# Turning the block-attention heads in 32x32 squares on VectorE, and moving one weight split, in a hybrid decoder block

## What is computed

```python
o_gla  = rms_norm(gla_chunked(...), gla_out_gain) * silu(gr)
o_moba = rms_norm(moba_attention(q_m, k_m, v), moba_out_gain)
x = x + concatenate([o_gla, o_moba]) @ w_out
h = rms_norm(x, norm2_gain)
x = x + (silu(h @ w_ffn_gate) * (h @ w_ffn_up)) @ w_ffn_down
return rms_norm(x, final_norm_gain)
```

## Time and profile before

| what | value |
|---|---|
| median of 3 runs | 301.15 us (300.92 to 301.44) |
| profiled execution | 301.26 us, of which the span of the trace is 299.5 us |
| TensorE busy | 292.4 us, 98% of the span |
| VectorE busy | 241.9 us, 81% |
| ScalarE busy | 170.4 us, 57% |
| GpSimd busy | 17.4 us, 6% |
| mean granted TensorE clock | 0.996 |

### The profile page before, as it was taken

One profiled execution on the slowest core, in us unless ns is written; L12 is line 12 of the kernel. 1 busy time (PEld: TensorE's weight loads), 2 busy tenths in 40 slices (PEclk: granted clock), 3 DMA queues, 4 the chain that ended last, 5 costly groups with the idle time before them and its releaser, 6 DMA issues.

```text
span 299.5 us, 4024 instructions
## 1 busy us (share of the span) xinstructions
PE 292.4 (98%) x1373; PEld 242.8 (81%) x1373; DVE 241.9 (81%) x402; ACT 170.4 (57%) x244; POOL 17.4 (6%) x41
## 2 busy tenths in 40 slices
PE   8999999999999999999999999999999999999992
PEld 7878888888898888888888888888888888888881
DVE  1999999877889687988888888888898978787155
ACT  3979798979765887717171718080808080813123
POOL 5210100000021001300000000000000000000011
PEclk9999999999999999999999999999999999999998
DMA  7997837837767122393939292929292929030003
GB/s 253 331 320 257 257 97 280 230 120 276 276 189 244 60 82 69 108 317 101 320 94 328 85 337 81 340 67 353 59 354 63 361 56 364 22 123 0 0 0 140
DMA packets 37382, 55.49 MB, mean 185 GB/s; under 512 B 2982, under 2 KB 26618, under 8 KB 37370
## 3 DMA queue, kind: packets, MB, share of 16 engines
q1 hardware_dynamic: 37204, 55.16, 54.6%
q10 hardware_dynamic: 166, 0.17, 0.2%
HBM read 53.75 MB, written 1.57 MB: 185 GB/s over the span
## 4 chain that ended last, share of the span: by engine, by line
PE 96%; DVE 1%; issue 1%; POOL 1%; ACT 0%; POOLq 0%; DVEq 0%
PE acc L515 15%; PE acc L517 15%; PE acc L516 15%; PE aux L517 13%; PE aux L516 13%; PE aux L515 13%; PE aux L618 1%; PE acc L532 1%; PE acc L569 1%; PE acc L572 1%; PE acc L575 1%; PE aux L688 1%; PE aux L541 1%; DVE x_sb L1388 1%; PE aux L712 1%
## 5 line engine op out<-in xcount | busy, mean ns | idle before, releaser
L1151 DVE TENSOR_TENSOR w_lo<-raw,w_hi 128x2048 fp32r<-128x2048 f32 x46 | 103.3, 2286 | 15.3 <-ACT w_hi L882 15.2
L882 ACT CAST w_hi<-raw 128x2048 fp32r<-128x2048 f32 x46 | 86.0, 1908 | 6.5 <-DMA raw<-in_w_in 2.9
L515 PE MATMUL aux<-w_hi,aT_hi 128*128 128x512 f32 (+1 forms) x180 | 69.7, 387 | 0.0
L517 PE MATMUL aux<-w_hi,aT_lo 128*128 128x512 f32 (+1 forms) x180 | 69.6, 387 | 0.0
L516 PE MATMUL aux<-w_lo,aT_hi 128*128 128x512 f32 (+1 forms) x180 | 69.6, 387 | 0.0
L1454 DVE STREAM_TRANSPOSE reuse_c<-reuse_c 32x128 f32<-32x128 f32 x160 | 48.4, 303 | 2.4
L1094 ACT CAST pT_hi<-reuse_c 128x512 fp32r<-128x512 f32 x10 | 6.2, 621 | 72.9 <-DVE reuse_c L1454 72.9
L515 PE MATMUL acc<-w_hi,aT_hi 128*128 128x512 f32 x118 | 47.1, 399 | 0.0
L517 PE MATMUL acc<-w_hi,aT_lo 128*128 128x512 f32 x118 | 46.0, 390 | 0.0
L516 PE MATMUL acc<-w_lo,aT_hi 128*128 128x512 f32 x118 | 46.0, 390 | 0.0
L515 PEld LDWEIGHTS aux<-w_hi,aT_hi 128*128 128x128 f32 x180 | 33.8, 188 | 6.9
(11 more groups left out here) (203 smaller groups left out, 283.8 us busy)
## 6 DMA issues: line engine op xcount, KB each, us to landing
raw<-in_w_ffn_gate SPq DMA_DIRECT2D x22, 512.0 KB, 4.0
raw<-in_w_ffn_up SPq DMA_DIRECT2D x22, 512.0 KB, 5.3
raw<-in_w_ffn_down SPq DMA_DIRECT2D x22, 512.0 KB, 5.9
raw<-in_w_in SPq DMA_DIRECT2D x20, 512.0 KB, 5.1
raw<-in_w_out SPq DMA_DIRECT2D x8, 512.0 KB, 4.4
raw<-in_w_in SPq DMA_DIRECT2D x8, 256.0 KB, 4.7
x_sb<-in_x SPq DMA_DIRECT2D x2, 512.0 KB, 3.8
m_moves<-reuse_c SPq DMA_DIRECT2D x1, 512.0 KB, 3.4
```

What stands on the lines that cost most here:

```text
L515: nc.tensor.matmul(dst, left_hi[:, k, tok], right_hi, start=first, stop=False)
L517: return nc.tensor.matmul(dst, left_lo[:, k, tok], right_hi, start=False, stop=last)
L882: nc.scalar.copy(w_hi[:, slot % RING, :], raw[:, slot % RAW, :]).then_inc(hi_ready, 1)
L1151: nc.vector.tensor_tensor(w_lo[:, slot % RING, :], raw[:, slot % RAW, :], w_hi[:, slot % RING, :].bitcast(f32), ALU.subtract).then_inc(lo_ ...
```

## The change

The eight TensorE transposes of the block-attention heads are gone. VectorE turns the squares of both tiles right after `normed`, ahead of split 15. For tile 0, ScalarE copies 8 blocks of 32x128 and GpSimd the other 8; for tile 1, ScalarE copies 12 and GpSimd 4. ScalarE makes the high parts and VectorE the low parts from SBUF, in new places of their orders. GpSimd's second inverse root comes behind its copies. Split 16 goes behind the block-attention heads on ScalarE, and behind the low part of gated tile 0 on VectorE. VectorE's wait for both activated gates becomes one wait for each tile.

```diff
+M_HEADS_MOVED_BY_POOL = (8, 12)
...
+        m_head_squares = reuse_e[:, 0:1024].rearrange("p (t c h i) -> p t c h i", t=T, c=QUADS, i=SQUARE)
+        m_headsT = reuse_e[:, 1024:2048].rearrange("p (t h s) -> p t h s", t=T, h=HEADS)
...
 # GpSimd
+            def move_m_heads(t, groups):
+                pool.wait_ge(m_heads_turned, t + 1)
+                for g in groups:
+                    for c in range(QUADS):
+                        nc.gpsimd.tensor_copy(m_headsT[SQUARE * c:SQUARE * (c + 1), t, :, SQUARE * g:SQUARE * (g + 1)],
+                                              m_head_squares[SQUARE * g:SQUARE * (g + 1), t, c, :, :]).then_inc(m_heads_by_pool, 1)
+                pool.wait_ge(m_heads_by_pool, M_HEADS_MOVED_BY_POOL[t])
+
+            head_root(0)
+            move_m_heads(0, (0, 1))
+            move_m_heads(1, (0,))
+            head_root(1)
...
 # TensorE
-                      9: [probs_transposed], 10: [moba_outputs, gla_updates], 11: [gla_outputs, lambda: heads_transposed(0, (3, 0))]}
+                      9: [probs_transposed], 10: [moba_outputs, gla_updates], 11: [gla_outputs]}
...
 # ScalarE
             split(15)
-            split(16)
...
+            def take_m_headsT(t):
+                act.wait_ge(m_heads_by_act, t + 1)
+                act.wait_ge(m_heads_by_pool, M_HEADS_MOVED_BY_POOL[t])
+                nc.scalar.mul(aT_hi[:, 0:HEADS, t * P:(t + 1) * P], m_headsT[:, t, :, :],
+                              gains[:, MOBA_ROW:MOBA_ROW + 1]).then_inc(headsT_hi_ready, 1)
...
+            move_m_heads(0, (2, 3))
             act.wait_ge(tile0_in_psum, len(BLOCKS))
             take_r(0)
+            take_m_headsT(0)
             act.wait_ge(ms_h_ready, 1)
             for t in range(T):
                 act.wait_ge(gla_in_psum, t + 1)
                 nc.scalar.activation(squares[:, t * W:(t + 1) * W], aux[:, 1 + t, :], ACT.Square).then_inc(sq_ready, 1)
-            take_headsT(0, (3, 0))
+            move_m_heads(1, (1, 2, 3))
             act.wait_ge(unit_used, IN_UNITS)
             take_r(1)
+            take_m_headsT(1)
+            split(16)
             split(17)
...
 # VectorE
                 normed(0, t, bank, o_moba[:, t, :, :]).then_inc(heads_ready, 1)
+            for t in range(T):
+                dve.wait_ge(heads_ready, t + 1)
+                nc.vector.transpose(m_head_squares[:, t], o_moba[:, t, :, :].rearrange("p h (c i) -> p c h i", c=QUADS)
+                                    ).then_inc(m_heads_turned, 1)
...
             split(15)
+            take_m_headsT(0)
             head_squares(1)
...
-            take_headsT(0, (3, 0))
-            split(16)
             dve.wait_ge(rstd_h_ready, 2)
-            dve.wait_ge(silu_r_ready, 2)
             normed(1, 0, 1, o_gla[:, 0, :, :])
             then(normed(1, 1, 2, o_gla[:, 1, :, :]))
             for t in range(T):
+                dve.wait_ge(silu_r_ready, t + 1)
                 nc.vector.tensor_tensor(o_gla[:, t, :, :], o_gla[:, t, :, :], silu_r[:, t, :, :], ALU.mult).then_inc(heads_ready, 1)
+            take_m_headsT(1)
...
             take_gla_headsT(0)
+            split(16)
             split(17)
```

More of the change, by code:

```diff
@@ L293, in build_block @@
         heads_ready = sem("heads_ready")
-        headsT_in_psum = sem("headsT_in_psum")
+        m_heads_turned = sem("m_heads_turned")
+        m_heads_by_act = sem("m_heads_by_act")
+        m_heads_by_pool = sem("m_heads_by_pool")
         heads_turned = sem("heads_turned")
@@ L489, in _, with head_root @@
             nc.gpsimd.memset(reuse_b[:, :], 0.0).then_inc(a_zeroed, 1)
-            for group in range(2):
+            def head_root(group):
                 pool.wait_ge(ms_h_ready, group + 1)
@@ L717, in gla_outputs @@
                     last.then_inc(gla_in_psum, 1)
[L719 to L724, removed]
             def out_product(t, group, n):
@@ L1001, in _, with move_m_heads @@
             split(15)
-            split(16)
[L1003 to L1010, removed]
+            def move_m_heads(t, groups):
+                act.wait_ge(m_heads_turned, t + 1)
+                for g in groups:
+                    for c in range(QUADS):
+                        last = nc.scalar.copy(m_headsT[SQUARE * c:SQUARE * (c + 1), t, :, SQUARE * g:SQUARE * (g + 1)],
+                                              m_head_squares[SQUARE * g:SQUARE * (g + 1), t, c, :, :])
+                last.then_inc(m_heads_by_act, 1)
+            def take_m_headsT(t):
[3 more added lines that the diff above has]
+                              gains[:, MOBA_ROW:MOBA_ROW + 1]).then_inc(headsT_hi_ready, 1)
             def take_r(t):
@@ L1343, in _, with take_m_headsT @@
                 normed(0, t, bank, o_moba[:, t, :, :]).then_inc(heads_ready, 1)
+            for t in range(T):
+                dve.wait_ge(heads_ready, t + 1)
+                nc.vector.transpose(m_head_squares[:, t], o_moba[:, t, :, :].rearrange("p h (c i) -> p c h i", c=QUADS)
+                                    ).then_inc(m_heads_turned, 1)
+            def take_m_headsT(t):
+                dve.wait_ge(headsT_hi_ready, t + 1)
+                dst = slice(0, HEADS), slice(t * P, (t + 1) * P)
+                lo_of_scaled(aT_lo[:, dst[0], dst[1]], m_headsT[:, t, :, :], gains[:, MOBA_ROW:MOBA_ROW + 1],
+                             aT_hi[:, dst[0], dst[1]]).then_inc(headsT_lo_ready, 1)
             split(15)
+            take_m_headsT(0)
             head_squares(1)
             nc.vector.tensor_scalar(ms_h[:, 1, :], ss_h[:, 1, :], 1.0 / DV, EPS, ALU.mult, ALU.add).then_inc(ms_h_ready, 1)
[L1348 to L1358 removed]
             dve.wait_ge(rstd_h_ready, 2)
[L1360 removed]
             normed(1, 0, 1, o_gla[:, 0, :, :])
```

8 lines of the change are left out of this document (removed).

## The result

| | before, same chip | after |
|---|---|---|
| median of 4 runs | 301.04 us | 306.19 us (306.00 to 306.46) |
| profiled execution | 301.26 us, span 299.5 | 306.00 us, span 303.9 |

The change makes the kernel slower: ratio 1.0166, 95% interval 1.0154 to 1.0178, or about 5.1 us. The sign and the mechanism are the forecast ones, the size is not: 2.8 us were forecast, and the time lies outside the range of 302.7 to 305.2.

A forecast was written before the change was run, and what follows sets the result against it. TensorE, 96% of the chain, was taken to bound the kernel: 0.87 us taken out, waits of 1.59, 1.29, 0.24, 0.29 and 0.27 put in, net +2.81, so 301.26 becomes 304.1 us, range 302.7 to 305.2.

The forecast's parts named there:

- The sign and the mechanism: Whole kernel: slower (chance 0.89), through held GpSimd with copies of 0.15 to 0.30 us, +2.3 to +3.6 us (chance 0.60).
- GpSimd's price: Tile 0's eight GpSimd copies: 0.20 us each, three before split 15, five from 88.51 to 89.51.
- The dearer rival at 0.29: GpSimd's tile 0 copies: two before the split, six left until 90.3; +3.6 us, 304.8; dearer copies had chance 0.10.
- ScalarE's queue: Ahead of the third block: ScalarE full from 91.23, gated tile 0's copies from about 99.7, TensorE starting at 103.52.
- my habit of the rows: Back-to-back instructions on one engine: the next starts about 0.09 us before the last has ended.
- The hold: Beside split 15: GpSimd instructions reading SBUF wait while VectorE subtracts two SBUF tensors, so five copies wait until 88.51.
- the slow root beside three splits: Profile before: GpSimd's one-element root took 2.49 us at 123.35 beside VectorE's splits, against 0.56 at 116.56.
- The deadlines: Starts of the four out_product blocks and tile 1's first gate product: slack before of 0.75, 5.5, 1.07, 0.95, 0.68 us.
- The rival by which only the first wait is real: Second low part not dependent in time on the gated norm: sum from -0.2 to +0.7 us, chance 0.07.
- The one by which GpSimd is not held: Tile 0's GpSimd copies not held or nearly free: high part at 88.70, +1.9 us, 303.2, chance 0.17.
- the later load: Unit 19's load: goes at about 105.7 instead of 92.55, lands by 111, wanted at 119.73 at the earliest, no cost.
- the later split 16: Split 16, ready at 105.7, is needed by the first gate product only after 115, so costs nothing.

The follow-up runs named there:

- split16_act_back: The changed kernel with ScalarE's split 16 back behind split 15, VectorE's order as changed: 305.32 us, ratio 1.0140 to the kernel before.
- split15_behind: The changed kernel with VectorE's split 15 moved behind the low part of block-attention tile 0: 305.49 us, ratio 1.0149 to the kernel before.
- split16_alone: The kernel before with only split 16 moved to its new places on ScalarE and VectorE, TensorE transposes kept: 300.98 us, ratio 0.9993.
- both_splits: The changed kernel with VectorE's split 15 behind tile 0's low part and ScalarE's split 16 back behind split 15: 306.15 us, ratio 1.0163 to the kernel before.
- gpsimd_half: The changed kernel with 4 of tile 0's copies on GpSimd and 12 on ScalarE, instead of 8 and 8: 305.64 us, ratio 1.0149 to the kernel before.

## Why the prediction was right in kind and short in size

The waits first. A wait is how much later a block starts than it would behind the block before it: 5.44 us after that, or, for the gate product, 11.73 (118.44 - 106.71). The first is counted from 90.39 - 0.87 - 0.34 = 89.18, as TensorE reaches the gated outputs 0.34 earlier in the profile after (83.74 for 84.08).

| wait at | forecast | measured | by the starts after |
|---|---|---|---|
| first block | 1.59 | 2.78 | 91.96 - 89.18 |
| second | 1.29 | 1.32 | 98.72 - 97.40 |
| third | 0.24 | 0.74 | 104.90 - 104.16 |
| fourth | 0.29 | 0.23 | 110.57 - 110.34 |
| gate product | 0.27 | 0.27 | 122.57 - 122.30 |
| sum | 3.68 | 5.34 | |

5.34 - 0.87 - 0.34 = 4.13, the lateness at the gate product. Two waits are mis-sized, the first by 1.19 and the third by 0.50; three are right. The table says when TensorE started, and not what each wait cost: a larger first wait leaves less for the next ones. What sets the end is the third block and what comes behind it.

*The step that failed: GpSimd's price.* "I take 0.20, as such instructions overlap a little", and from it three copies before the split and five held, done at 89.51. Measured: 0.28 to 0.30 each and 0.34 from start to start; two free, one held through the split, five behind it, done at 90.27. They don't overlap, they stand 0.06 apart. VectorE begins this stretch 0.16 earlier in the profile after (83.65 for 83.81), so the high part, forecast at 89.60, began at 90.36 + 0.16 = 90.52: 0.92 of the 1.19. Five copies at 0.34 instead of 0.20 make 0.7 of it; the rest is mostly that the held copy ends 0.16 after the split. A further 0.18 is that TensorE had come 0.34 earlier and VectorE only 0.16, and 0.10 is the restart below. The dearer rival at 0.29 had the number of copies right and forecast 304.8; it had no time between them.

The rows for a better price were there, but not for the right one. The select reads and writes and took 0.29; the memset only writes. Of the overlap the whole timeline before says, one row ahead of the select shown:

```profile
3.25 0.29 POOL L460 TENSOR_SCALAR_AFFINE_SELECT tri_mid<-tri_mid 128x128 fp32r<-128x128 f32 x1
```

Selects start 0.24 to 0.25 apart (3.25, 3.49, 3.74). At 0.25 five held copies would end at 89.76, and the sum at 304.3. No row before has the 0.34. The copies raise a semaphore each and these selects do not; whether that makes the difference was not tested.

*The second failed step, at the third wait: ScalarE's queue.* From the high part of tile 0 to the gated copies 10.14 were summed (89.60 to about 99.7) and 10.35 measured (90.36 to 100.71): the two squarings 0.10 more, the twelve copies 0.05, the two splits 0.10. Then the high part of gated tile 0 began 0.09 after its last copy had ended (100.71 + 2.45 = 103.16 against 103.25), where my habit of the rows had it 0.09 before: it waits for copies of its own engine. The sum itself lost 0.08 in rounding: 99.74 + 2.44 is 102.18, not 102.1. That is how 0.92 at tile 0 became 1.40 at the low part of gated tile 0 (104.01 + 0.75 + 0.16 = 104.92 for 103.52). That this queue is the releaser was shown by split16_act_back, and the chain runs through it; the single joins were only read from the timeline.

*TensorE's restart.* After each wait the first matmul began 0.10 to 0.15 after the low part had ended (91.96 against 91.11 + 0.75). I had let it start at once. A block that starts after a pause also takes 5.57 (91.96 to 97.30 + 0.23) instead of 5.44; the table counts these 0.13 with the next wait.

*The hold was right.* Reading the slow root beside three splits as a GpSimd instruction held by VectorE's subtraction came true in its place: 2.24 for one copy under split 15, none of twelve held where no split ran beside them. The Trainium skill's SBUF — State Buffer, section "Who interferes with whom", names this pair, and the trace agrees. The Trainium skill's GPSIMD Engine Reference, section "Performance versus the Vector engine", would have made a copy cheaper still than my 0.20; here the measured 0.34 decides.

*The deadlines were right, in order and in releaser.* The second block, which had 5.5 us of slack before, waits for a low part that stands behind the norm of the gated heads. split15_behind showed it: its first block starts 1.5 earlier than in the change, its second does not. The rival by which only the first wait is real fell with that. The one by which GpSimd is not held fell with the 2.24.

*At no cost, as forecast:* the later load, the later split 16 (split16_alone), GpSimd's four copies for tile 1.

*Outside the forecast.* VectorE's last instruction is 3.98 later. The span, to the hundredth, ends 4.03 after that starts (303.87 - 299.84), for 3.68 before (299.54 - 295.86). This 0.35 is no scatter: the four kernels in which GpSimd makes twelve copies (the change, split15_behind, split16_act_back, both_splits) have 4.02 or 4.03, the other fourteen, gpsimd_half with eight among them, 3.66 to 3.68, each in its one profile. At the end of the program SyncE waits 0.5 for TensorE's sequencer in these four, and 0.2 in all the others. Why is open. The time outside the span is 0.41 more in these two executions (306.00 - 303.87 for 301.26 - 299.54), which I had taken as fixed. 3.98 + 0.35 + 0.41 = 4.74, the difference of the two profiled executions. The profiled one of before lay 0.22 above its median and that of after 0.19 below, which makes the 5.15 between the medians. So of the 1.93 by which the profiled execution missed the forecast of 304.07, 1.17 lies in the waits, as far as they reach VectorE's last instruction, and 0.76 behind it.

## What to carry to other kernels

Before trading TensorE work for copies elsewhere, write down the slack at every block that TensorE starts: where a left side is ready only 0.75 us ahead, taking 0.87 off TensorE can't return it all. Then follow the chain and not the largest gap: here the largest gap, ended 1.5 us sooner, gave back 0.7, while one cast moved out of ScalarE's full queue gave back 1.0 with that gap hardly touched. Price a small copy on GpSimd from start to start, by an instruction that reads, writes and raises a semaphore, and where no row has one, let the range reach well above the nearest. In this kernel it should not stand beside a VectorE instruction with two SBUF inputs. A late input moves along the hand-written orders: a wait that is removed at one block comes back at the next unless the whole chain is shorter.

## What the runs showed of the hardware that was not expected

- A GpSimd copy of 32x128 float32 with a semaphore takes 0.29 us and the next starts 0.34 after it; held by a VectorE subtraction, one takes 2.24 (tile view: median 286 ns, longest 2236), and under VectorE's low part another takes 0.66. It goes both ways: where the low part starts under a running copy, it takes 0.84 instead of 0.75 (split15_behind, both_splits).
- TensorE's granted clock fell to half in two kernels, 0.3 us after it had started again from a pause of 2.11 and 1.4 us after one of 3.13, for seven or eight matmuls, and stayed full in the change after 2.63. The length of the pause alone doesn't decide it.
- The time outside the span has two values, 1.75 and 2.12 or so, by whether VectorE executes 402 instructions or more. The time from VectorE's last instruction to the end of the span has two as well, 3.67 and 4.03, by whether GpSimd makes all twelve copies, in one profile of each kernel. Both causes are open.
